# Norm statistics on VectorE instead of GpSimd, and a new order of small operations around them, in a fused two-block transformer kernel

## What is computed

```python
# first block
x = x + concat(rms(moba(qa, ka, va)), diff(qb, kb, vb)) @ w_out   # q,k,v = rms(x) @ w_in, relative bias tables
x = x + memory_cross_attention(rms(x), rms(mem))                  # w_cq, w_ck, w_cv, w_co
x = x + (silu(h @ w_gate) * (h @ w_up)) @ w_down                  # h = rms(x, ffn_norm_g)
x = rms_norm(x, final_norm_g)
# second block, layers 0 and 1
h = rms(x, mix_norm[i]); x = x + (attn_conv_mixer(h) if i == 0 else gla_mixer(h))
x = x + conv_ffn(rms(x, ffn_norm[i]))
x = x + sigmoid(rms(x, ple_norm[i]) @ w_gate) * (p[i] @ w_proj)

def rms_norm(x, g):
    return x * rsqrt(mean(x * x, axis=-1) + 1e-6) * g
```

## Time and profile before

| | us |
|---|---|
| median of 3 runs | 1135.23 |
| lowest and highest | 1131.5, 1135.26 |
| the profiled execution, its own time | 1134.79 |
| its span in the trace | 1133.0 |
| TensorE busy (97%) | 1095.1 |
| VectorE busy (74%) | 837.5 |
| ScalarE busy (54%) | 612.7 |
| GpSimd busy (5%) | 59.2 |

### The profile page before, as it was taken

How to read it: one execution, slowest core, us unless ns; L and a number is a source line. 1 busy time by engine, 2 the same in 40 slices (tenths; PEclk the granted TensorE clock), 3 DMA queues, 4 the chain that set the end, 5 groups by cost and what they waited for, 6 DMA issues and landing times.

```text
span 1133.0 us, 21949 instructions
## 1 busy us (share of the span) xinstructions
PE 1095.1 (97%) x8800; PEld 1066.6 (94%) x8800; DVE 837.5 (74%) x1055; ACT 612.7 (54%) x798; POOL 59.2 (5%) x41
## 2 busy tenths in 40 slices
PE   6999999999999998999999999998999999999998
PEld 5979999999999998987999999997999999999997
DVE  6658776566666746898788897476887879889456
ACT  6656652555444436546666665364546566665452
POOL 1200010010000002000100000022000100000020
PEclk9999999999999999999999999999999999999999
DMA  8933364435555562532555456544332545555641
GB/s 310 228 112 112 116 212 156 149 123 182 179 177 178 192 211 108 186 112 83 182 183 180 169 179 225 187 167 139 130 142 75 186 149 186 182 178 181 225 169 41
DMA packets 29417, 186.38 MB, mean 165 GB/s; under 512 B 3511, under 2 KB 5784, under 8 KB 7592
## 3 DMA queue, kind: packets, MB, share of 16 engines
q1 hardware_dynamic: 29352, 185.45, 47.9%
HBM read 184.09 MB, written 1.34 MB: 164 GB/s over the span
## 4 chain that ended last, share of the span: by engine, by line
PE 79%; DVE 11%; DMA 4%; ACT 3%; issue 2%; SPq 0%; DVEq 0%; ACTq 0%
PE g L451 55%; PE d L451 24%; DVE w_lo L1184 4%; DMA raw<-weights 3%; DVE a_lo L1188 1%; ACT w_hi L835 1%; DVE b_lo L1188 1%; PE d L454 1%; DVE x L1181 1%; ACT hy_scores L835 1%; DMA bias_dram<-bias_rows 0%; DVE newton L1178 0%; DVE newton L1188 0%; SPq L412 0%; DVE x L1188 0%
## 5 line engine op out<-in xcount | busy, mean ns | idle before, releaser
L1184 DVE TENSOR_TENSOR w_lo<-raw,w_hi 128x2048 fp32r<-128x2048 f32 (+1 forms) x171 | 389.0, 2278 | 95.7 <-ACT w_hi L835 95.5
L835 ACT ACTIVATE w_hi<-raw 128x2048 fp32r<-128x2048 f32 (+1 forms) x171 | 323.5, 1896 | 127.7 <-PE d L451 90.2
L451 PE MATMUL g<-a_hi,w_hi 128*128 128x256 f32 x1232 | 356.7, 290 | 17.2 <-DVE w_lo L1184 11.1
L451 PE MATMUL g<-a_lo,w_hi 128*128 128x256 f32 x1232 | 350.0, 284 | 0.0
L451 PE MATMUL g<-a_hi,w_lo 128*128 128x256 f32 x1232 | 349.9, 284 | 0.0
L451 PEld LDWEIGHTS g<-a_hi,w_hi 128*128 128x128 f32 x1232 | 237.5, 193 | 25.1 <-DVE w_lo L1184 12.6
L451 PEld LDWEIGHTS g<-a_lo,w_hi 128*128 128x128 f32 x1232 | 237.6, 193 | 0.1
L451 PEld LDWEIGHTS g<-a_hi,w_lo 128*128 128x128 f32 x1232 | 237.5, 193 | 0.0
L451 PE MATMUL g<-b_hi,w_hi 128*128 128x256 f32 x672 | 192.3, 286 | 5.1 <-DVE w_lo L1184 4.3
L451 PE MATMUL g<-b_lo,w_hi 128*128 128x256 f32 x672 | 190.4, 283 | 0.0
L451 PE MATMUL g<-b_hi,w_lo 128*128 128x256 f32 x672 | 190.4, 283 | 0.0
(11 more groups left out here) (270 smaller groups left out, 1343.9 us busy)
## 6 DMA issues: line engine op xcount, KB each, us to landing
raw<-weights SPq DMA_DIRECT2D x169, 1024.0 KB, 4.9
bias_tab<-bias_dram SPq DMA_DIRECT2D x8, 192.0 KB, 9.2
x<-x_t SPq DMA_DIRECT2D x4, 256.0 KB, 6.3
raw<-weights SPq DMA_DIRECT2D x2, 512.0 KB, 5.8
mem_t<-mem_t SPq DMA_DIRECT2D x1, 1024.0 KB, 13.2
out<-x SPq DMA_DIRECT2D x4, 256.0 KB, 2.3
p_in<-p_t SPq DMA_DIRECT2D x2, 256.0 KB, 5.1
level_mask_f<-level_mask SPq DMA_DIRECT2D x1, 512.0 KB, 5.3
```

The source lines that it names most:

```text
L451: return pe.matmul(out, lhsT, rhs, start=start, stop=stop, skip_group_check=True)
L835: return act.activation(out, in_, func, **kw)
L1184: return dve.tensor_tensor(out, a, b, ALU.subtract)
```

## The change

1. The squares of the four pairs go to four tiles (`sq_sum`, `sq[0]`, `sq[1]`, `newton`), so ScalarE waits for no addition. VectorE adds them (three additions of 128x512) and folds the two halves (one of 128x256). GpSimd keeps its memsets, of which those for gla_in now wait for `x_gated`.
2. `norm_sum` is one matmul over 256 columns instead of two that accumulate, and stands behind chunk 1 in place of chunk 0 (in gla_in between the low-rank matmuls and chunk 1; behind chunk 0 still in the gate phases). The gain norm of hy_in gets bank `D[2]`.
3. `opening(name)`: both low (high) halves of chunks 2 and 3 are made before the norm's own steps; the first two evictions no longer have one behind them.
4. `residual` is now add, residues, `ahead`, sums. `down` makes residues between its additions, the last `ahead` after them, then the sums.
5. The memory's norm: its sums stand ahead of eviction 6, its matmul behind the first score tiles, its scale behind the first softmax's normalisation; its low halves are made 4 and 4.
6. gate1: residues before `ahead`; the halves of `gla_wlr` are made at its chunk 1; the low-rank result has a semaphore of its own.

```diff
@@ TensorE
-            def norm_sum(sums=sq_sum):
+            def norm_sum(squares=SQUARES, bank=STAT):
 
                 pe.wait_ge(sq_total, count.next(sq_total))
-                acquire(STAT)
-                mm(D[STAT][:, 0:T], ones, sums[:, 0:T], True, False)
-                fill(STAT, mm(D[STAT][:, 0:T], ones, sums[:, T:2 * T], False, True), full_dve, mean_done)
+                acquire(bank)
+                fill(bank, mm(D[bank][:, 0:T], ones, squares[0][:, 0:T]), full_dve, mean_done)
...
-            turn_scale(rstd_mem, W_IN_Q + 1)
+            norm_sum()
             for j in (7, 8):
                 chunk("w_in", j, j % U, A)
+            turn_scale(rstd_mem, W_IN_Q + 2)
...
                 chunk("hy_in", j, j % U, A, fresh=j == 0)
-                if j < 2:
-                    norm_sum((sq_sum, gain_sq_sum)[j])
+                if j == 1:
+                    norm_sum()
+                    norm_sum(GAIN_SQUARES, 2)
...
@@ ScalarE
+            def opening(name):
+
+                ahead(name, 0, 0)
+                ahead(name, 1, 1)
+                rough_rstd()
...
-            for j in range(W_IN_Q):
-                ahead("w_in", j, j % U)
-                if j == 0:
-                    rough_rstd()
+            opening("w_in")
+            for j in range(1, W_IN_Q):
+                if j > 1:
+                    ahead("w_in", j, j % U)
                 if j == 1:
                     from_bank(bias_rows[0:ATT_HEADS, :], D[0][0:ATT_HEADS, 0:N_DIST])
...
             ahead("w_in", 7, 1)
+            rough_rstd()
             weigh_values(8, 4, probs_t, att_a, square_of(att_a))
@@ VectorE
+            def add_squares(first, last, squares=SQUARES):
+
+                for i in range(first, last):
+                    dve.wait_ge(sq_done, count.next(sq_done))
+                    if i > 1:
+                        dve.wait_ge(dve_own, count.sent[dve_own])
+                    if i > 0:
+                        add(squares[0], squares[0], squares[i]).then_inc(dve_own, count.one(dve_own))
+
+            def halve_squares(squares=SQUARES):
+
+                dve.wait_ge(dve_own, count.sent[dve_own])
+                add(squares[0][:, 0:T], squares[0][:, 0:T], squares[0][:, T:2 * T]).then_inc(sq_total, 1)
+
+            def opening(name):
+
+                ahead(name, 0, 0)
+                ahead(name, 1, 1)
+                token_norm()
...
                     add(pair, pair, bank_of(name, j, j % U)).then_inc(evicted, count.one(evicted))
-                    ahead(name, j, j % U)
                     dve.wait_ge(evicted, count.sent[evicted])
                     prep_pair(moving, gain, g0, x, j)
+                    ahead(name, j, j % U)
+                    add_squares(j, j + 1)
+                halve_squares()
...
                     add(pair, pair, as_tiles(D[b][:])).then_inc(x_ready, count.one(x_ready))
+                    if b > 0:
+                        prep_pair(moving, gain, g0, x, b - 1)
                 dve.wait_ge(x_ready, count.sent[x_ready])
+                prep_pair(moving, gain, g0, x, 3)
+                ahead(name, COUNT[name] - 1, (COUNT[name] - 1) % U)
+                add_squares(0, KT // 2)
+                halve_squares()
...
+                    if layer == 1 and j == 1:
+                        dve.wait_ge(lr_hi_done, count.next(lr_hi_done))
+                        sub(flat(gla_wlr_lo), flat(gla_wlr), flat(gla_wlr_hi).bitcast(F32)).then_inc(lr_split, 1)
```

More of the change, by code:

```diff
@@ L366, in head_squares @@
             return sq[:, b, :] if b < 2 else flat(gla_w[1])[:, (b - 2) * 2 * T:(b - 1) * 2 * T]
+        SQUARES = [sq_sum[:], sq[:, 0, :], sq[:, 1, :], newton[:]]
+        GAIN_SQUARES = [gain_sq[:, i, :] for i in range(KT // 2)]
         block = stack.enter_context(nc.Block())
@@ L865, in prep_pair, with squares @@
                 squares(i, src)
[L867 to L871, removed]
+            def squares(i, src, to=SQUARES, gain=None):
+                to = to[i]
                 if gain is None:
@@ L982, in _ @@
             residual("w_out", C, "cross_norm_g")
-            for j in range(COUNT["w_cq"]):
+            opening("w_cq")
+            for j in range(2, COUNT["w_cq"]):
                 ahead("w_cq", j, j % U)
-                if j == 0:
-                    rough_rstd()
             exps(scores_mem, 0, 8, slice(0, T))
@@ L1012, in gated_body @@
             def gated_body(j, jm):
-                ahead("up0", j, jm)
-                if isinstance(j, int) and j == 0:
-                    rough_rstd()
+                early = isinstance(j, int)
+                if early and j == 0:
+                    opening("up0")
+                elif not early or j > 1:
+                    ahead("up0", j, jm)
                 act.wait_ge(gate_done, count.next(gate_done))
@@ L1079, in body @@
                     early = isinstance(j, int)
-                    ahead(name, j, jm)
                     if early and j == 0:
-                        rough_rstd()
+                        opening(name)
+                    elif not early or j > 1:
+                        ahead(name, j, jm)
                     act.wait_ge(evicted, out_count(name, j))
@@ L1299, in first_chunk @@
                 else:
-                    evict("w_in", j, j % U, pair_at(qkv, j))
+                    evict("w_in", j, j % U, pair_at(qkv, j), split=j > 1)
             for j in range(W_IN_Q):
@@ L1387, in _ @@
             residual("w_out", C, "cross_norm_g")
+            opening("w_cq")
             for j in range(COUNT["w_cq"]):
-                if j == 0:
-                    token_norm()
-                evict("w_cq", j, j % U, pair_at(q_mem, j))
+                evict("w_cq", j, j % U, pair_at(q_mem, j), split=j > 1)
             for b in range(4):
@@ L1416, in hidden_lo, with down @@
                 sub(tile_at(hid_lo, j), ring[:, jm % U, :], tile_at(hid_hi, j).bitcast(F32)).then_inc(hid_split, 1)
-            def down(layer, between=None, first=0):
+            def down(layer, moving, gain, g0=0, between=None, first=0):
                 name = f"down{layer}"
@@ L1483, in gated_body @@
                     hidden_lo(j - 2, jm + 1, hid)
-                ahead("up0", j, jm)
+                if not early or j > 1:
+                    ahead("up0", j, jm)
             count.each(FT, gated_body)
@@ L1489, in _ @@
             hidden_lo(FT - 1, (FT - 1) % U, hid)
-            down(0, rope_angles)
-            prep(A, both_g)
-            ahead("down0", FT // 2 - 1, (FT // 2 - 1) % U)
+            down(0, A, both_g, 0, rope_angles)
             def hy_evict(j, split=True):
@@ L1648, in conv_ffn @@
                 sub(flat(p_lo), flat(p_in), flat(p_hi).bitcast(F32)).then_inc(p_split, 1)
-                down(layer, first=1)
-                ahead(f"down{layer}", FT // 2 - 1, (FT // 2 - 1) % U)
-                prep(ple_moving, "ple_norm_2", (layer - 1) * KT)
+                down(layer, ple_moving, "ple_norm_2", (layer - 1) * KT, first=1)
                 gate = f"gate{layer}"
@@ L1684, in gla_evict @@
                                     ALU.mult, ALU.mult).then_inc(evicted, count.one(evicted))
-                    ahead("gla_in", j, j % U)
+                    if j == 1:
+                        ahead("gla_in", j, j % U)
                 elif 4 <= j < 8:
```

104 lines of the change are left out of this document (44 added, 60 removed).

## The result

The changed kernel takes 1136.87 us (median of 12 runs, 1134.8 to 1139.04), the kernel before 1134.09 (12 runs, 1131.5 to 1135.28): a ratio of 1.0026, 95% interval 1.0015 to 1.0038. The profiled execution took 1136.06, with a span of 1134.2.

A forecast was written before the change was run, and what follows sets the result against it. TensorE, busy 97% of the span, was taken as the bound, with VectorE releasing it. Terms 7.3 - 3.6 - 1.6 + 1.5 - 4.3 = -0.7 led to a forecast of 1134.5 us, range 1128 to 1140.

The forecast's parts named there:

- w_in, +7.3: First phase: 2.0 us for a later load, 2.65 for the mem norm's sums, 2.65 for its scale; bounds 5.5 and 9.5.
- the bound of +1: In w_in, the low bound for the 1 MB chunk's later landing: all shared queue work absorbed, +1 us where +2.0 was taken.
- The idle stretch of 2 to 3 us: In w_in, a sign: TensorE idle 2 to 3 us ahead of the transposes after chunk 8, showing the scale term.
- rival A: Faster, 1129: w_in terms mostly hidden, +2 in place of +7.3, the landing moving 1 us instead of 2; chance 0.27.
- Halved norms and two low halves ahead, -3.6: In w_cq, up0, up1, up2 and gate2: half a norm sum saved, shorter residue waits in four; bounds 2 and 5 us.
- down0 to hy_in, -1.6: Residues done earlier, chunk 3 waiting 2.4 us, giving -3.2, less 1.6 for half clock behind that wait; bounds -4 and 0.
- My own sign of being wrong: The prediction was to be wrong if hy_in gained nothing, or if w_in ended less than 4 us later than before.
- hy_out, +1.5: At hy_out's start, a_hi and two residues stand ahead of chunk 2's low half, delaying TensorE; bounds 0 and +2 us.
- gate1 to gla_in, -4.3: Low-rank wait and its half clock go, residues quicken, 1.0 us returned by the low half behind residues; bounds -5 and -1.5.
- B: Slower, 1141: late bias rows delay w_in's loads, TensorE waits 4.4 us longer and its clock falls again; chance 0.11.
- C: 1137: the change misses its purpose, residues staying at 1.5 us; hy_in gains 2.0 less, gate1 0.5 less; chance 0.07.
- D: 1136.6: gate1's memsets slow two pairs of residues by up to 1.0 us each, +2; chance 0.09.

The follow-up runs named there:

- e5: The changed kernel with four matmuls of constants in the wait between hy_in's two groups of score tiles: 1134.65 us, ratio 1.0005 to the kernel before.
- e9: The changed kernel with matmuls of constants in three long waits (two in hy_in, one in gate1), none in w_in: 1133.76 us, ratio 0.9995 to the kernel before.
- e8: The kernel before with matmuls of constants in two waits, at w_in's score tiles and ahead of the low-rank matmuls: 1132.37 us, ratio 0.9989.
- e4: The changed kernel's order and tiles, with the norm sums on GpSimd instead of VectorE: 1139.18 us, ratio 1.0047 to the kernel before.
- e1: The changed kernel with the memory's norm moved back ahead of the scores, additions still on VectorE: 1131.38 us, ratio 0.9975 to the kernel before.
- e11: A repeat of the changed kernel with five orders mended (memory norm, bias rows, gate1, hy_out, hy_in's cast) and no filling: 1127.93 us, ratio 0.9944.
- e2: The changed kernel with ScalarE's copy of the bias rows ahead of rough: 1134.60 us, ratio 1.0003 to the kernel before.
- e7: The changed kernel with five orders mended (memory norm, bias rows, gate1, hy_out, hy_in's cast) and no filling: 1126.00 us, ratio 0.9939.
- e3: The changed kernel with the old order in gate1's middle chunks, low halves ahead of residues: 1135.45 us, ratio 1.0007 to the kernel before.
- e10: The changed kernel with memory norm, bias rows, gate1 and hy_out orders mended, and matmuls of constants in two hy_in waits: 1124.50 us, ratio 0.9919.

## Why the prediction was wrong

**The sum.** The sign failed by terms that were each small. By the traces +1.3 stands against my -0.7; hy_in alone is 1.65 of the 2.0 between them.

- *w_in, +7.3: right in place and nearly in size.* The load landed 1.2 later and not 2.0. That is not because the copy moved less: in e5 and e9, with the same order, it moved by 2.8 and 3.2 and the load landed at 52.39 and 52.58. So most of the delay was absorbed, the case that I had as the bound of +1; and in e8, with the old order, the load landed at 52.45, so 1 us lies within what executions differ by. With the sums the score tiles were released at 62.94, 3.8 later (forecast 4.65, "near 64"), and the transposes came 6.2 later, not 7.3: the landing is what was mis-sized. The idle stretch of 2 to 3 us that I named as a sign ahead of the transposes is 0.21, as half clock (63.4 to 70.3) stretched the two chunks ahead of it. e4 confirms the 2.65 of the sums; e1, 6.0 us shorter in w_in, that the place cost nearly all of it. It was the largest term, and I gave rival A, its absence, 0.27, although the chain of the earlier trace rows spoke against it.
- *Halved norms and two low halves ahead, -3.6: measured -3.0.* w_cq, up0 and gate2 as said; up1 gave 0.22 and up2 0.53 in place of 0.8. In up1 a new wait of 0.47 for a low half (at 588.84) stands against it.
- *down0 to hy_in, -1.6: measured +0.05, the step that failed.* My own sign of being wrong, that hy_in gains nothing, came. Its parts of work came nearly as worked out. Chunk 0 ends 5.75 behind down0's last matmul in place of 10.88, and chunk 3 starts at 467.03, 20.9 behind it in place of 23.9: 3.0 sooner where I had 3.2, by a wait of 2.26 where I had 2.4:

```profile
466.19 0.70 DVE hy L1182
...
467.03 5.98 PE g L453 x48
```

What failed is the term for the loss of clock, in place and in size. I booked 1.6 behind this new wait and nothing behind any old one; behind the new one none came in this execution. It came 33 us later, behind a wait of 1.94 that the kernel before has too, with no half clock behind it then: 3.0 us, of which e5 shows 2.4 to count (about the rest comes back as the 0.5 on the way to hy_out: without half clock, in e5, that way is as long as before). "I take that here too", behind the wait that the change makes, was the faulty step: any wait of that size can have it, old ones too. The 1.6 itself was no bad price: in e11 and e2 half clock did come behind this wait, and cost 1.5 in each (hy_in is 1.56 shorter than before in e11, 3.06 in e7, which has the same order and no half clock there). It came in two of the seven traces in which the wait is not filled, so a single execution may or may not have it.
- *hy_out, +1.5: measured +1.53.* The chain has the low half behind the residues:

```profile
538.37 0.88 DVE a_lo L1192 x2
539.25 2.21 DVE w_lo L1188
...
541.50 18.50 PE g L453 x152
```

- *gate1 to gla_in, -4.3: measured -3.1.* The wait for the low-rank weights and their half clock went, as said. The low half behind residues gives back 1.1 (e3), near the 1.0 booked: the high half of the low-rank weights, a_hi, the residues and their low half now all stand ahead of it, and TensorE waits longer than in any place of gate1 before:

```profile
772.82 0.38 PE L453 MATMUL g<-b_hi,w_hi 128*128 128x256 f32 x1 [2.32 <-DVE w_lo L1188]
...
790.04 0.70 PE L453 MATMUL d<-sq_sum,const 128*128 128x256 f32 x2 [1.12 <-DVE sq_sum L1185]
```

The second row is nearly all of the 1.2 that is missing. The last pair's sums are still being made on VectorE when the low-rank matmuls end, and TensorE waits 1.12 for them ahead of the norm matmul; before it did not wait there. I had put the sums at nothing in this phase, and booked half a norm sum as gained. e3 and e5 have the same wait (1.10 each).

**The base.** I forecast from a median of 1135.23 of three runs; twelve gave 1134.09. Of the 2.8 us, 1.5 are neither in my terms nor in the two traces, but in how these executions stand to their medians. With a scatter of 4 us from run to run, which the clock explains in part (in the change 0.988 to 0.994, or 6.8 us), a term-by-term sum could not have been sure of the sign.

**The rivals.** A did not come: w_in is +6.3 and not +2, though the landing moved by the 1 us that it had. B did not come either: the load landed at 52.58, below the 55 that B required. The half clock behind the longer wait, its second part, came, but beside the chain. C fell by the residues' 478 ns. D fell as well: the longest memset ran beside a pair of residues, on GpSimd's timeline and on VectorE's, and the pair still took 0.88.

```profile
764.24 1.38 POOL L1886 MEMSET gla_s<- 128x1536 f32 x1 [763.40 <-DVE x L1185]
```

```profile
764.77 0.88 DVE L1192 SCALAR_TENSOR_TENSOR a_lo<-x,par,a_hi 128x256 fp32r<-128x256 f32 x2 [0.66 <-ACT a_hi L834]
```

I had also read from a mean of 2290 ns that low halves do not suffer beside additions. The mean hid it: with the additions spread otherwise, in e4, low halves take up to 3.38 us.

By the Trainium skill's rule (GPSIMD Engine Reference, section Specifications), VectorE's instructions with two SBUF inputs contend with GpSimd for the SBUF interfaces that the two share. The traces agree beside GpSimd's additions, for residues (1.56 in e4) and for low halves (3.38), and show no contention beside its memset, which has no input (0.44 a residue).

## What to carry to other kernels

Moving a small operation to the engine where it is short is not enough; what it stands ahead of decides: one norm, sums and scale, cost 6 us more ahead of evictions that the chain runs through than a few places earlier, where 0.8 was left. Count every wait of TensorE of the sizes that had half clock behind them here (1.55 us in e10 to 4.73 us in the change) twice, once for itself and once as a chance of half clock behind it, in waits that the change does not touch too; a few matmuls of constants in such a wait are a cheap test of that. And look what else runs beside the slow stretch before booking its price: in the change's w_in up to the transposes, and in gate1, it cost nothing; in hy_in nearly all; and in w_in once more nearly all (1.5 of 1.7) in the old order and in the mended one. When another engine's chain is mended, the clock begins to count.

## What the runs showed of the hardware that I had not expected

The same wait brings half clock in one execution and none in another. hy_in's wait of 1.93 to 1.94 us, unchanged in length, was followed by about 7 us with a clock of 0.5 in the profiles of the change, e2, e3 and e4, and by none in those of the kernel before, e1, e7, e8 and e11. In the first four it ended at 498.5 us or later, in the others at 498.3 or earlier. Whether that is chance or a matter of when the wait falls is open; no run tried it. Over 12 runs of one binary the mean clock went from 0.993 to 1.000 (e1) and the time from 1127.59 to 1133.07 with it.
